# The second attention's scores in fp32r: queries stacked high over low, keys' high and then low parts moving

## The reference

```
kband, vband = with_prev(kb), with_prev(vb)
s_band = jnp.einsum('bnqkgd,bnskd->bnkgqs', qb, kband, ...) * scale + bias_band
s_band = jnp.where(mask_band[None, :, None, None], s_band, NEG)
k_meta, v_meta = k[:, PAD:BLOCK], v[:, PAD:BLOCK]
s_meta = jnp.einsum('bnqkgd,bmkd->bnkgqm', qb, k_meta, ...) * scale + bias_m[None]
p = jax.nn.softmax(jnp.concatenate([s_meta, s_band, sink], axis=-1), axis=-1)
out = einsum(p_meta, v_meta) + einsum(p_band, vband)
y_att = att @ w_attn_branch
```

## Time and profile before

| | |
|---|---|
| median of 3 runs | 2361.61 us (2360.47 to 2362.68) |
| profiled execution | 2362.93 us, its span 2361.1 us |
| PE busy | 2335.4 us, 99% |
| DVE busy | 1470.8 us, 62% |
| ACT busy | 874.2 us, 37% |
| POOL busy | 182.9 us, 8% |
| mean granted clock of PE | 0.996 of full |
| the eight blocks | from 1679.67 us (first score) to about 1876 us |

### The profile page before, as it was taken

How to read it: one execution, slowest core, us unless ns; L and a number is a source line. 1 busy time by engine, 2 the same in 40 slices (tenths; PEclk the granted TensorE clock), 3 DMA queues, 4 the chain that set the end, 5 groups by cost and what they waited for, 6 DMA issues and landing times.

```text
span 2361.1 us, 35543 instructions
## 1 busy us (share of the span) xinstructions
PE 2335.4 (99%) x14487; PEld 2035.5 (86%) x14487; DVE 1470.8 (62%) x2597; ACT 874.2 (37%) x1385; POOL 182.9 (8%) x259
## 2 busy tenths in 40 slices
PE   9999999999999999999999999999999999999998
PEld 6888888888877778888879999999999999998997
DVE  6556344354767745445468977887677656873784
ACT  4123122132548832222245772774333333221212
POOL 0000000000028700000001200210100000000000
PEclk9999999999999999999999999999999999999999
DMA  5237323424352213222223522542222222223223
GB/s 176 91 89 148 107 89 117 140 98 122 108 146 74 76 54 107 90 89 93 102 89 112 120 76 102 115 108 90 91 82 82 80 90 90 89 89 125 90 100 113
DMA packets 67621, 239.11 MB, mean 101 GB/s; under 512 B 22482, under 2 KB 33170, under 8 KB 43634
## 3 DMA queue, kind: packets, MB, share of 16 engines
q1 hardware_dynamic: 31044, 200.14, 25.0%
q0 software_dynamic: 5952, 18.44, 4.2%
q10 hardware_dynamic: 30496, 18.73, 3.6%
HBM read 228.41 MB, written 10.09 MB: 101 GB/s over the span
## 4 chain that ended last, share of the span: by engine, by line
PE 85%; DVE 8%; issue 2%; POOL 2%; ACT 2%; DMA 1%; SPq 0%; DVEq 0%; ACTq 0%; POOLq 0%
PE ps L1159 44%; PE ps L1470 24%; PE ps L1761 5%; PE ps L1581 4%; DVE wlo L1816 2%; POOL Sb L544 1%; PE ps L1396 1%; PE ps L1416 1%; DMA raw<-in_stream 1%; PE ps L1663 1%; DVE Pb L2530 1%; PE ps L1341 1%; PE ps L1691 1%; PE ps L1286 0%; ACT Sb L901 0%
## 5 line engine op out<-in xcount | busy, mean ns | idle before, releaser
L641 ACT ACTIVATE whi<-raw 128x2048 fp32r<-128x2048 f32 (+2 forms) x182 | 340.1, 1869 | 823.3 <-PE ps L1159 427.2
L1816 DVE TENSOR_TENSOR wlo<-raw,whi 128x2048 fp32r<-128x2048 f32 (+3 forms) x213 | 418.6, 1966 | 68.8 <-ACT whi L641 67.4
L1159 PE MATMUL ps<-parts,whi 128*128 128x512 f32 x1328 | 419.2, 397 | 2.0 <-DVE ct L1960 2.0
L1470 PE MATMUL ps<-parts,whi 128*128 128x258 f32 (+1 forms) x2400 | 404.2, 290 | 1.1 <-issue 0.8
L1470 PEld LDWEIGHTS ps<-parts,whi 128*128 128x128 f32 x2400 | 331.4, 189 | 11.9 <-issue 10.0
L1159 PEld LDWEIGHTS ps<-parts,whi 128*128 128x128 f32 x1328 | 249.0, 189 | 63.5 <-issue 4.6
L1159 PE MATMUL ps<-parts,wlo 128*128 128x512 f32 x664 | 263.3, 397 | 0.0
L1470 PE MATMUL ps<-parts,wlo 128*128 128x258 f32 (+1 forms) x1200 | 242.5, 284 | 0.0
L1159 PE MATMUL ps<-Mlo,whi 128*128 128x512 f32 x512 | 203.0, 396 | 0.0
L1159 PE MATMUL ps<-Mhi,whi 128*128 128x512 f32 x512 | 203.0, 396 | 0.0
L1159 PE MATMUL ps<-Mhi,wlo 128*128 128x512 f32 x512 | 203.0, 396 | 0.0
(11 more groups left out here) (420 smaller groups left out, 3873.6 us busy)
## 6 DMA issues: line engine op xcount, KB each, us to landing
raw<-in_stream SPq DMA_DIRECT2D x186, 1024.0 KB, 4.8
csb<-sums_d POOLq DMA_DIRECT2D x16, 512.0 KB, 6.0
bands<-scratch ACTq DMA_DIRECT2D x7, 1024.0 KB
csf<-sums_d POOLq DMA_DIRECT2D x32, 128.0 KB, 6.0
tabs<-bands ACTq DMA_DIRECT2D x8, 418.0 KB, 4.5
X<-in_x SPq DMA_DIRECT2D x4, 512.0 KB, 7.0
near_a<-bands ACTq DMA_DIRECT2D x8, 256.0 KB, 2.9
Q_odd<-parts POOLq DMA_DIRECT2D x8, 256.0 KB, 4.4
```

The lines of the kernel that those rows point to most:

```text
L641: nc.scalar.activation(whi[:, s, 0:cols], raw[:, s, 0:cols], ACT.Copy).then_inc(hi_done, 1)
L1159: mm = nc.tensor.matmul(out, w[:, s, at], x(k), start=k + j == 0, stop=k == k_tiles - 1 and j == 2)
L1470: mm = nc.tensor.matmul(ps[:, 2 * par + h, 0:w], wt[:, s, at], x[:, k, a + h * w:a + (h + 1) * w], start=k + j == 0, stop=k == k_tiles - 1 ...
L1816: low = nc.vector.tensor_tensor(wlo[:, s, a:b], raw[:, s, a:b], whi[:, s, a:b].bitcast(F32), ALU.subtract)
```

## The change

Scores become sums of two fp32r matmuls. The stationary operand is the new `QS[:, h]`: for head h its 64 rows hold the high part of that head's queries, and the other 64 rows the low part of the same queries. `keys2[:, 0]` holds the keys' high part in both halves, `keys2[:, 1]` the low part in both. One matmul with each, accumulated in PSUM, gives (high + low) of the queries times (high + low) of the keys. Q2 is now the tile `acc`. The moving pieces are one column wider (274, 146 and 18), and in six scores of nine DVE reads its row one column further on. ACT makes the high part of the queries (two copies of 64 rows), DVE subtracts for the low part, and PE waits for that. The first head's keys are staged on DVE by two copies and two subtractions, the second's by two copies on ACT and two subtractions on GpSimd. PE does its last k-steps of a block before the values' matmuls instead of behind them, and DVE takes the next queries out of PSUM at the end of a block instead of at the start of the next.

```diff
-                Q2 = sb("Q2", [P, TOK], F32, scope)
+                Q2, QS = acc, sb("QS", [P, 2, TOK], F32R, scope)
...
+            own_keys, meta_keys = key_columns(1)
+            pool.wait_ge(k_hi, 2 * GROUPS + 1)
+            nc.gpsimd.tensor_tensor(keys2[:, 1, :, ROW0:], own_keys, keys2[:, 0, :, ROW0:].bitcast(F32), ALU.subtract).then_inc(k_lo, 1)
+            nc.gpsimd.tensor_tensor(keys2[:, 1, :, 1:ROW0], meta_keys, keys2[:, 0, :, 1:ROW0].bitcast(F32), ALU.subtract).then_inc(kv_staged, 1)
...
+                    act.wait_ge(mt_free, i * 12 + (T0["pair"] + 3 * p + 1))
+                    act.wait_ge(s2_full, i * 36 + 9 * p)
+                    for h in range(2):
+                        rows = slice(h * DH, (h + 1) * DH)
+                        nc.scalar.activation(QS[rows, h, CUT:], Q2[rows, CUT:], ACT.Copy).then_inc(q_hi, 1)
                     if p % 2:
                         next_unit("pair", 3 * p // 2, turn=i * 6, half_turn=i * 3)
...
-                            mm = nc.tensor.matmul(ps[:, 4, 0:2 * ROW0], Q2[:, 0:P], keys2[:, :, 0, 0:ROW0], start=True, stop=True)
+                            for h in range(2):
+                                for part in range(2):
+                                    mm = nc.tensor.matmul(ps[:, 4, h * (ROW0 + 1):(h + 1) * (ROW0 + 1)], QS[:, h, 0:P], keys2[:, part, 0, 0:ROW0 + 1],
+                                                          start=part == 0, stop=part == 1)
...
-                            mm = nc.tensor.matmul(ps[:, 4 + n % 2, 0 if c > 1 else P:ROW], Q2[:, at:at + P], keys, start=True, stop=True)
+                            for part in range(2):
+                                row = keys2[:, part, :, :].rearrange("p c n -> p (c n)")
+                                keys = row[:, (c - 2) * ROW1 + ROW0 - 1:c * ROW1] if c > 1 else row[:, 0:ROW1 + 1]
+                                mm = nc.tensor.matmul(ps[:, 4 + n % 2, 0 if c > 1 else P:ROW + 1], QS[:, h, at:at + P], keys, start=part == 0, stop=part == 1)
...
-                    pe.wait_ge(mt_free, i * 12 + (T0["pair"] + 3 * p + 1))
+                    pe.wait_ge(q_lo, KT + 2 * (i * 4 + p) + 2)
...
                     turn_meta()
-                    dense(1)
+                    dense(len(steps))
                     values_first()
                     values()
                     values_meta()
-                    dense(len(steps))
...
+            def queries_low(i, p):
+                k = i * 4 + p
+                for h in range(2):
+                    own_rows, other = slice(h * DH, (h + 1) * DH), slice((1 - h) * DH, (2 - h) * DH)
+                    dve.wait_ge(q_hi, KT - 2 + 2 * k + h + 1)
+                    nc.vector.tensor_tensor(QS[other, h, CUT:], Q2[own_rows, CUT:], QS[own_rows, h, CUT:].bitcast(F32), ALU.subtract).then_inc(q_lo, 1)
...
-                    if i * 4 + p != 4:
-                        queries(i, p)
+                    if i + p == 0:
+                        queries(0, 0)
+                    queries_low(i, p)
...
+                    if p < 3:
+                        queries(i, p + 1)
                     first_out()
                     if p == 3:
                         gate_att()
                         if not i:
-                            dve.wait_ge(first_full, 4)
                             queries(1, 0)
+                            dve.wait_ge(o2_full, 4)
                             values_staged(1)
                         split_low("pair", 5, i * 6)
```

More of the change, by code:

```diff
@@ L308, in program @@
                 Pmeta = sb("Pmeta", [P, P], F32, scope)
-                Pfirst = sb("Pfirst", [P, P], F32, scope)
+                Pfirst = causal
                 PT2 = sb("PT2", [P, 2, (2 * QT - 1) * P], F32, scope)
@@ L435, in of_round, with key_columns @@
             return g, 2 * (r // 4) + r % 2, r // 2 % 2
+        def key_columns(i):
+            keys = t_at(Kd2, i)
+            return keys[:, N_META:].rearrange("p (c n) -> p c n", c=QT), keys[:, 0:N_META].unsqueeze(1).to_broadcast([P, QT, N_META])
         def near_of(h):
@@ L1073, in _ @@
                         act.wait_ge(s2_full, 36)
[L1074 to L1079, removed]
+                        own_keys, meta_keys = key_columns(1)
+                        nc.scalar.activation(keys2[:, 0, :, ROW0:], own_keys, ACT.Copy)
+                        nc.scalar.activation(keys2[:, 0, :, 1:ROW0], meta_keys, ACT.Copy).then_inc(k_hi, 1)
             act.wait_ge(mt_free, T0["att"])
@@ L2465, in _ @@
                         split_low("half", r // 2, i * 14)
-            own.mark(nc.vector.memset(keys2[:, :, :, :], 0.0))
+            own.mark(nc.vector.memset(keys2[:, :, :, :].bitcast(F32), 0.0))
             own.mark(nc.vector.memset(Pfirst[:, :], 0.0))
-            own.mark(nc.vector.memset(Q2[:, 0:CUT], 0.0))
+            own.mark(nc.vector.memset(QS[:, :, 0:CUT].bitcast(F32), 0.0))
             nc.vector.tensor_scalar(gate_h[:, :], vec("gate_b", 0, 2 * KT), 0.5, None, ALU.mult).then_inc(gate_half, 1)
@@ L2493, in queries @@
                 nc.vector.scalar_tensor_tensor(halves(Q2[:, CUT:]), late_product(3 * p % 2), DH ** -0.5, halves(R[:, CUT:]), ALU.mult, ALU.mult).then_inc(mt_free, 1)
[L2495 to L2499, removed]
+            def queries_low(i, p):
[4 more added lines that the diff above has]
+                    nc.vector.tensor_tensor(QS[other, h, CUT:], Q2[own_rows, CUT:], QS[own_rows, h, CUT:].bitcast(F32), ALU.subtract).then_inc(q_lo, 1)
+            own_keys, meta_keys = key_columns(0)
+            own.mark(nc.vector.tensor_scalar(keys2[:, 0, :, ROW0:], own_keys, one, None, ALU.mult))
+            own.mark(nc.vector.tensor_scalar(keys2[:, 0, :, 1:ROW0], meta_keys, one, None, ALU.mult))
+            own.wait()
+            nc.vector.tensor_tensor(keys2[:, 1, :, ROW0:], own_keys, keys2[:, 0, :, ROW0:].bitcast(F32), ALU.subtract)
+            nc.vector.tensor_tensor(keys2[:, 1, :, 1:ROW0], meta_keys, keys2[:, 0, :, 1:ROW0].bitcast(F32), ALU.subtract)
             values_staged(0)
@@ L2514, in softmax_in @@
                         at, a, b = (0, 0, ROW) if n > 1 else (P, ROW, ROW + ROW1)
-                        nc.vector.tensor_tensor_reduce(Pb[:, n, at:], ps[:, 4 + n % 2, at:ROW], tabs[:, n % 2, a:b], -1.0, -2 * MASKED,
+                        shift = int(n > 1)
+                        nc.vector.tensor_tensor_reduce(Pb[:, n, at:], ps[:, 4 + n % 2, at + shift:ROW + shift], tabs[:, n % 2, a:b], -1.0, -2 * MASKED,
                                                        ALU.add, ALU.min, nmax2[:, n % 2:n % 2 + 1]).then_inc(ttr2, 1)
```

6 lines of the change are left out of this document (2 added, 4 removed).

## The result

| | before | after |
|---|---|---|
| median of the runs | 2361.61 us (22 runs, 2360.47 to 2364.97) | 2365.82 us (22 runs, 2364.87 to 2368.99) |
| span of the profiled execution | 2361.1 us | 2363.1 us |
| ratio to before | | 1.0017, 95% interval 1.0011 to 1.0023 |

A forecast was written before the change was run, and what follows sets the result against it. TensorE, busy 99% of the span, was taken as the bound. Terms -8.1 + 1.6 + 3.4 + 2.5 + 3.2 = +2.6 us gave 2364.2 us for the median, range 2358.8 to 2369.0.

The forecast's parts named there:

- scores: PE's score matmuls in all eight blocks: fp32r pairs replace f32, ninth score loses; 1.01 us gained per block, 8.1 in all.
- waits in odd blocks: Blocks 1, 3, 5, 7: splits make DVE late and transposes wait 0.4 us, four times, 1.6 us in all.
- start of block 0: PE waits 3.7 us for the query chain, one subtraction held by GpSimd; 3.4 us net, bounds 2.3 and 4.7.
- change of key head: Block 4's start: subtractions queue on DVE behind values and split; PE waits 3.2 us, 2.5 net, bounds 2.0 and 3.2.
- clock: PE's clock falls behind both long waits, 1.7 us each; 3.2 us net of small hidden waits, bounds 0 and 7.
- even blocks change nothing: Blocks 0, 2, 4, 6: transposes that wait come behind the longer ninth score, so no change was counted.
- The third rival: Clock stays low longer after both waits and both block 0 subtractions meet GpSimd: +7.7 us, 2369.3 us; chance 0.17.
- The first rival: Waits come, but the clock stays at 2.4 GHz and no subtraction meets GpSimd: -1.7 us, 2359.9 us; chance 0.16.
- the second: Query chain hidden at block 0 and at the head change, about 1 us of waits left: 2354.5 us; chance 0.06.
- the fourth: Matmuls of 146 and 274 columns in fp32r run at the f32 pace: about 2372 us; chance 0.03.

The follow-up runs named there:

- experiment 3: Changed kernel, with the second half split of odd blocks moved from step 2 to step 4: 2363.54 us, ratio 1.0008.
- Experiment 4: Changed kernel, with each score again one f32 matmul and the keys' low part left out of the scores: 2373.05 us, ratio 1.0048.
- experiment 2: Changed kernel, with GpSimd's eight products of X held back until block 1's low queries exist: 2365.69 us, ratio 1.0016.
- experiment 5: Changed kernel, with ScalarE scaling X ahead of its next split and GpSimd taking each tile as it comes: 2362.68 us, ratio 1.0001.
- experiment 1: Changed kernel, with DVE subtracting block 4's low queries ahead of the values' staging and the whole unit's split: 2362.08 us, ratio 1.0002.
- experiment 6: Changed kernel, with three more dense k-steps ahead of the first score in blocks 0 and 4, three fewer behind: 2359.18 us, ratio 0.9984.
- experiment 7: Changed kernel: block 4's low queries first, X scaled early, odd splits at step 4, block 0's values staged after the queries' product: 2357.40 us, ratio 0.9979.

## Why the prediction was right, and where it was off

The forecast's sum, with what the traces of after and the experiments put in the place of each term:

| term | forecast | measured | from |
|---|---|---|---|
| scores | -8.1 | -8.1 | 1.05 x 4 even, 0.98 x 4 odd (25.44 to 24.46, experiment 3) |
| waits in odd blocks | +1.6 | +1.5 | 0.38 x 4, experiment 3 |
| start of block 0 | +3.4 | +4.1 | idle 4.32 for 0.26 |
| change of key head | +2.5 | +2.5 | wait +3.05, less 0.55 inside block 4 |
| clock | +3.2 | +3.5 | 1.0 in block 0, 2.5 in block 4 |
| sum | +2.6 | +3.5 | the profiled executions; medians: +4.2, by the ratio 4.0 |

The clock's row takes blocks 0 and 4 as even blocks (24.83 without disturbance): block 0 took 1.5 and block 4 2.65 more. Before, they took 0.53 and 0.70 more than an even block's 25.88, in waits of their first softmax; block 4's is counted in the term of the key head but for 0.15.

**The scores.** Width no longer pays at 18 and 146 columns, as read from the 64-column row. The term was right to 0.1 us in sum, with the ninth score a little cheaper than forecast (0.36 us for 0.43). Experiment 4 puts the gain in the scores and not in the new order: with f32 scores in the new order no block was shorter than before the change (25.89 us for 25.88, 25.6 for 25.44). The eight ordinary scores of a block were priced at 1.24 + 0.06 = 1.30 us; by this experiment they bring 1.06, net of waits, in even blocks and 1.14 in odd ones without the wait (25.6 less 24.46).

**DVE behind the shorter step.** The wait came at step 4 of odd blocks, and taking one split away from it ended it. That even blocks change nothing was right in sum: their transposition behind the ninth score was late by 0.3 us both before and after.

**Block 0.** This is the step that was mis-sized. I took one of the two subtractions as held by GpSimd and priced it from a one-source row. Both were: 3.28 us for 1.41, 1.9 us and not 1.1. Experiments 2 and 5 end the hold in two different ways and both give 1.41. The rule quoted from the Trainium skill, "SBUF — State Buffer", section on the engine ports, was the better guide: each operation of this kind that began while GpSimd's products ran was held here. One that had begun just ahead of them was not: in experiment 5 a whole split begun at 1665.22 took its usual 2.29 us, with GpSimd's first product from 1665.27.

**The key head.** Right in place, cause and size; experiment 1 took it away by order alone. I had priced the split and not asked whether it had to stand there.

**The clock.** It fell behind both waits, and experiment 6 shows that the waits were the cause. Its length was mis-sized in block 4, 6.8 us for 3.6. The third rival's mechanism was thus half there: one long stretch of two, and both subtractions held. With both stretches long the time would have been near 2366.7 (0.9 us more, an estimate from block 0's 27.21 us in experiment 1 and 26.36 in after). What decides between 3.4 and 6.8 us I can't say: the same wait of block 0 gave 3.4 in after and 6.8 in experiment 1, and the same wait of block 4 gave 6.8 in after and 3.4 in experiment 3 (block 4 lasted 26.37 us there for 27.48).

The first rival fails on the clock and on the held subtractions, the second on both waits, the fourth on the 0.25 us of a score.

## What to carry to other kernels

A saving on the engine that bounds the kernel is only kept where the others have slack for it: here 8.1 us of matmul time were saved, about 1 in every block, and two block starts and one badly placed split took 12 back. When an operand gets one more preparation step, list each place where nothing stands ahead to hide it, and put the new step first in its engine's queue there, before work that nobody waits for yet. In these runs all but one of the waits of 2 to 4.3 us on TensorE at a block start brought the clock down and cost some 1 to 3 us beyond their length; such a wait should be counted so, and any ready matmul put into it.

## What the runs showed of the hardware

- TensorE's clock behind a wait is not settled by the wait's length near 2 us: it fell after 1.99 us of idle (experiment 7, and 1.97 in the earlier trace rows) and not after 2.23 (experiment 6). Behind all waits of 2.46 us and more at blocks 0 and 4 it fell, for 3.4 or 6.8 us.
- Blocks with a stretch of 3.4 us lasted some 1.5 us longer than an undisturbed even block of 24.83 (block 0: 26.36 us in after, 26.47 in experiment 2; block 4: 26.37 in experiment 3), and those with one of 6.8 us 2.4 to 2.9 longer (block 0: 27.21 in experiment 1, 27.32 in experiment 3, 27.77 in experiment 5; block 4: 27.48 in after). In block 0 some 0.5 of it is not the clock's: at full clock in experiment 6 it took 23.12 us with three k-steps of 0.73 fewer, which makes 25.3 by estimate.
- Beside GpSimd's products VectorE's operations from SBUF to SBUF take about twice as long or more: two subtractions 3.28 us for 1.41, a half split 2.30 for 1.22, a scaling 1.27 for 0.36. One that takes an operand from PSUM kept its 0.68. GpSimd's own eight products took 10.06 us in experiment 2 and 12.14 in experiment 5, by where they lay.
- An fp32r matmul of 18 columns costs PE almost as much as one of 146: four take 0.36 and 0.40 us, start to start. One of 274 columns costs 0.13 (a pair 0.25 to 0.26).
